# Even attention: where four state-space low parts and four evictions of turned probabilities run

## The reference, cut to what matters

```python
att = swa_sink_attention(q, k, v, sinks, rel_bias) * silu(gate_a)    # 8 heads, window of 128
ssm = s5_mixer(u, ...) * silu(gate_b)                                # state space, then a gated unit
return concatenate([att, ssm]) @ w_out

# inside the attention, for each block of 128 queries
logits = where(mask, q @ k.T * scale + bias, -1e30)
p   = softmax(concatenate([logits, sink]))[..., :-1]
out = p @ v
# inside the mixer
y = gelu(y);  h = y @ glu_w + glu_b
return h[..., :W] * sigmoid(h[..., W:])
```

## Time and profile before

| | us |
|---|---|
| median of 3 runs | 2011.0 (2010.79 to 2011.02) |
| the profiled execution | 2010.99 |
| its span, from first to last instruction | 2009.7 |
| busy: TensorE, VectorE, ScalarE, GpSimd | 1944.4, 1438.2, 882.5, 620.8 |
| mean granted clock of TensorE, of full speed | 0.993 |

### The profile page before, as it was taken

How to read it: one execution, slowest core, us unless ns; L and a number is a source line. 1 busy time by engine, 2 the same in 40 slices (tenths; PEclk the granted TensorE clock), 3 DMA queues, 4 the chain that set the end, 5 groups by cost and what they waited for, 6 DMA issues and landing times.

```text
span 2009.7 us, 24201 instructions
## 1 busy us (share of the span) xinstructions
PE 1944.4 (97%) x9108; PEld 1504.4 (75%) x9108; DVE 1438.2 (72%) x2198; ACT 882.5 (44%) x1573; POOL 620.8 (31%) x428
## 2 busy tenths in 40 slices
PE   8999989999999999999999999999999999999997
PEld 6777867787548787666787887888777877777785
DVE  7668686522379997455357799899997887685639
ACT  5343285333457751545212333544226764352431
POOL 3554410552101122545352000000003673235443
PEclk9999999999999999999999999999999999999999
DMA  6322330442501122311333211111142223455322
GB/s 271 128 72 83 114 123 22 167 158 69 151 22 33 53 76 82 105 42 53 123 98 105 74 54 63 53 53 53 57 147 86 79 74 145 163 191 195 112 85 105
DMA packets 72428, 197.90 MB, mean 98 GB/s; under 512 B 11182, under 2 KB 20559, under 8 KB 71800
## 3 DMA queue, kind: packets, MB, share of 16 engines
q1 hardware_dynamic: 72168, 196.35, 28.9%
q10 hardware_dynamic: 144, 0.00, 0.0%
HBM read 152.89 MB, written 46.71 MB: 99 GB/s over the span
## 4 chain that ended last, share of the span: by engine, by line
PE 47%; DVE 30%; ACT 4%; issue 3%; DMA 2%; POOL 1%; SPq 0%; DVEq 0%; ACTq 0%
PE psum L266 44%; DVE m L2973 10%; DVE m L2187 4%; PE psum L269 3%; DVE m L2994 2%; DVE m L321 2%; DMA m<-in_w 1%; POOL m L311 1%; ACT m L301 1%; DVE m L540 1%; DVE m L456 1%; DVE m L531 1%; DVE m L3172 1%; DVE m L3111 1%; DVE m L3175 1%
## 5 line engine op out<-in xcount | busy, mean ns | idle before, releaser
L266 PE MATMUL psum<-m,m 128*128 128x512 f32 (+10 forms) x8308 | 1862.1, 393 | 40.1 <-DVE m L321 9.8
L266 PEld LDWEIGHTS psum<-m,m 128*128 128x128 f32 (+4 forms) x8308 | 1418.6, 186 | 454.0 <-issue 137.7
L311 POOL TENSOR_TENSOR m<-m,m 128x1024 fp32r<-128x1024 f32 (+1 forms) x122 | 307.9, 2527 | 1002.3 <-ACT m L301 1002.2
L301 ACT ACTIVATE m<-m 128x1024 fp32r<-128x1024 f32 (+2 forms) x166 | 173.4, 1048 | 342.1 <-PE psum L266 208.5
L2973 DVE SCALAR_TENSOR_TENSOR m<-m,m,m 128x1024 f32<-128x1024 f32 x240 | 312.3, 1303 | 6.3
L269 PE MATMUL psum<-m,m 128*128 128x128 f32 x784 | 110.6, 277 | 12.1 <-ACT m L1450 6.1
L269 PEld LDWEIGHTS psum<-m,m 128*128 128x128 f32 x784 | 89.6, 141 | 33.3 <-ACT m L1450 8.0
L2187 DVE TENSOR_SCALAR_CACHE_REDUCE m<-m,m 128x896 bf16<-128x896 f32 (+4 forms) x130 | 102.8, 847 | 1.1
L2519 POOL TENSOR_TENSOR m<-m,m 128x384 f32<-128x384 f32 (+5 forms) x48 | 72.5, 1528 | 55.9 <-DVE m L2311 37.2
L2407 ACT ACTIVATE m<-m,m 128x1024 bf16<-128x1024 f32 (+1 forms) x62 | 64.1, 1035 | 26.4 <-DVE m L2214 26.4
L2311 DVE CUSTOM_DVE_ANT_0 m<-psum,m 128x128 f32<-128x128 f32 (+3 forms) x64 | 48.3, 755 | 37.9 <-PE psum L266 36.7
(11 more groups left out here) (314 smaller groups left out, 1652.9 us busy)
## 6 DMA issues: line engine op xcount, KB each, us to landing
m<-in_w SPq DMA_DIRECT2D x164, 512.0 KB, 3.7
scr_hscr<-m SPq DMA_DIRECT2D x4, 2048.0 KB, 6.6
m<-scr_hscr SPq DMA_DIRECT2D x4, 2048.0 KB, 10.6
scr_turned<-scr_strip SPq DMA_DIRECT2D x8, 575.5 KB, 12.6
m<-in_x SPq DMA_DIRECT2D x4, 1024.0 KB, 7.9
scr_gscr<-m SPq DMA_DIRECT2D x16, 256.0 KB, 4.2
m<-in_x SPq DMA_DIRECT2D x2, 2048.0 KB, 8.8
m<-scr_turned SPq DMA_DIRECT2D x8, 512.0 KB, 4.5
```

The costliest lines, as they stand in the source:

```text
L266: return self.nc.tensor.matmul(out, lhsT, rhs, start=start, stop=stop, skip_group_check=True)
L301: k.nc.scalar.activation(k.hi[SLOT[i]][:, 0:kk * n], k.raw[i % 2][:, 0:kk * n], ACT.Copy).then_inc(*k.up("w_hi", i))
L311: k.nc.gpsimd.tensor_tensor(lo, raw, hi.bitcast(F32), ALU.subtract).then_inc(*k.up("w_lo", i))
```

## The change

Two things are moved.

1. `low_y` goes from VectorE to GpSimd. It was in VectorE's steps 6 to 9, at the end of the step; it is now in GpSimd's loop, in steps 5 to 8, behind the weight panel of step 4. It still waits for `y_hi(m)` of ScalarE.
2. The eviction of block c = 1 of units 4 to 7 goes from ScalarE to VectorE, in steps 6 to 9. There it stands behind `s1b` and ahead of `s3`, and waits for the transposes (`swa_PT_ps`) and for `swa_O` of two units before. ScalarE keeps block 0 of those units, and both blocks of all others.

```diff
+        self.turned_by_dve = [(i - 2, 1) for i in range(6, 10)]
...
 (vector_even)
-    def low_y(m):
-        dve.wait_ge(*at("y_hi", m))
-        V.tensor_tensor(E.YL[:, m], E.YT[m].rearrange("p j c -> p (j c)"), E.YH[:, m].bitcast(F32), ALU.subtract).then_inc(*up("y_lo", m))
+    def s2(b, p):
+        i = E.units.index((b, p))
+        for c in range(E.band(b)[0] // 128):
+            if (i, c) not in E.turned_by_dve:
+                continue
+            dve.wait_ge(*at("swa_PT_ps", b, p, c))
+            dve.wait_ge(*at("swa_O", *E.units[i - 2]))
+            V.tensor_copy(E.PT[i % 2][:, c, :], k.bank(E.PB[(b, p, c)])).then_inc(*up("swa_PT", b, p, c, also=[("free", "ev_PB", b, p, c)]))
...
             s1b(*E.units[i - 1])
+        if 2 <= i <= n + 1:
+            s2(*E.units[i - 2])
         if i >= 3:
             s3(*E.units[i - 3])
-        if i - 1 in E.y_steps:
-            low_y(E.y_steps.index(i - 1))
...
 (scalar_even, s2)
+            if (i, c) in E.turned_by_dve:
+                continue
             act.wait_ge(*at("swa_PT_ps", b, p, c))
...
 (pool_even)
+    def low_y(m):
+        pool.wait_ge(*at("y_hi", m))
+        G.tensor_tensor(E.YL[:, m], E.YT[m].rearrange("p j c -> p (j c)"), E.YH[:, m].bitcast(F32), ALU.subtract).then_inc(*up("y_lo", m))
...
         if E.late_panel(i):
             pool_panel(k, 14 + E.late_panel(i))
+        if i in E.y_steps:
+            low_y(E.y_steps.index(i))
```

## The result

The changed kernel took 2022.0 us (median of 4 executions, 2018.7 to 2023.6) beside 2011.0 for the kernel before (2010.8 to 2012.6): a ratio of 1.0048, 95% interval 1.0036 to 1.0061. The profiled execution took 2023.56.

The account below looks back on a forecast made before the run. TensorE bounds the kernel, but ahead of the gated unit VectorE's steps 6 to 9 set its start; GpSimd's low parts holding VectorE add 3.8 + 1.65 + 1.41 = 6.9 us to 2010.99, giving 2017.9 us, range 2014.5 to 2020.5.

Parts of the forecast that it names:

- the level: Whole kernel: the starting time the forecast adds to, 2010.99 us from the profiled execution, with a median of 2011.0.
- the sum: L1177 of step 9 and the gated unit: 3.8 + 1.65 + 1.41 = 6.9 us later, 2017.9 us; chance 0.54.
- The copy: VectorE, steps 6 to 9: the PSUM copy adds 0.61 us a step, runs beside GpSimd and makes nobody wait.
- Step 6: VectorE: two low parts hold L1188 (L1189 after the change); copy 4.4 us late, step 7's L1177 3.8 late.
- Steps 7 to 9: VectorE: each low part holds L1177 back, 6.35 us a step against 4.70 and 4.94, so 1.65 and 1.41 more.
- without a gap: Kernel before, steps 7 to 9: VectorE never waits, so it sets the step of 4.70 and 4.94 us.
- The turn that passes only at the end of the four: Rival, step 6: GpSimd gets in only after all four L1188; +4.5 us, 2015.5 us; chance 0.15.
- L1189 unheld: Rival, step 6: this one-input operation (L1188 before) is not held; +3.7 us, 2014.7 us; chance 0.08.
- Low parts that hide: Rival, steps 6 to 9: low parts run beside L1170, the copy and L1194; -1.8 us, 2009.2 us; chance 0.08.
- The clock at half in the gated unit's first products: Rival, TensorE from `glu`'s start, turnings too: half clock makes it +9 to 10 us, 2020 to 2021; chance 0.15.
- the hold: VectorE, steps 6 to 9: a low part on GpSimd holds SBUF operations up to 2.27 us, depending on its start.

Follow-up runs that it names:

- the low parts alone: Against the kernel before, only the low parts moved to GpSimd, both evictions left on ScalarE: 2018.1 us, ratio 1.0027.

## Why the prediction was wrong, point by point

**What failed is the last step, the level.** "2010.99 + 6.9 = 2017.9" set the difference on three executions that agreed within 0.23 us; the clock stood in the sum at nothing, and in the range at "up to 2 or 3 us". Those three lay 2.3 us under the mean of 77; an unchanged kernel moves by 10 us between its extremes, with the half-clock stretches that an execution takes; and the four executions of the first comparison lay 0.9 us above the mean of the changed one's 14. The 11.0 us of that comparison against the pooled 7.4 are these things. In the profiled execution the stretches at 63, 391 and 503 us, far from the change, added 4.5 us. No row of one trace could have shown the level, but the earlier trace rows showed that such stretches exist, and I priced the one beside the change and not those of the other 2000 us. The range should have reached some 3 us further up for that alone. Why the first three agreed so well stays open: of the 73 later executions of the kernel before, three picked at random lie within 0.23 us in 0.3% of cases, so it was rare luck or something particular to that first measurement, whose chip isn't on record.

**The difference held, its main term a little high.**
- *The copy*: 0.68 beside GpSimd's work and alone, and without the low parts' move +0.58, +0.59 and +0.35 us in three steps (8.06, 5.29 and 5.29 where 7.48, 4.70 and 4.94 were), with nothing held: as said.
- *Step 6*: the first of the four was held to 290.03, and the low part of 290.17 got its turn between the second and third L1189, as the earlier trace rows had suggested for L1213. Step 6 to 7 took 10.90 us instead of 7.48, +3.4 where I had +3.8: two of the four had run before the second low part's turn, where I had allowed for one or two, and the copy came 4.0 us late, not 4.4.
- *Steps 7 to 9*: 6.33 and 6.32 us where I had 6.35; +1.63 and +1.38 where I had 1.65 and 1.41. (The terms as written, 3.9 + 2.27 + 0.20, make 6.37; the slip is 0.02 us.)
- The sum, 6.43 against 6.9, reached the gated unit in full, and behind it nothing caught up. The held operations are those of the forecast, and the times of the low parts too to 0.5 us, after the 1.45 us by which this execution was late before it; VectorE's busy time went up by 5.0 us.
- *A misreading that cost nothing*: VectorE isn't "without a gap" in the kernel before. In step 8 it waited for TensorE's product, which is most of the 0.24 us by which that step is longer:

```profile
297.03 0.42 DVE L1194 TENSOR_TENSOR m<-psum,m 128x256 f32<-128x256 f32 x1 [0.16 <-PE psum L266]
```

**The rivals.** The turn that passes only at the end of the four fell (it passed after two), and so did L1189 unheld (2.21 us). Low parts that hide are no fault of the idea: with one wait they do hide, and the prediction's figure for that case, -1.8, came out at -1.5 in the trace. What stood against it, that ScalarE's start is tied to L1177 and sets the bad phase anew each step, was right for the change as made. The clock at half in the gated unit's first products did come, in one of three profiles of the changed kernel, and with the size forecast: the stage added 9.2 us there, where I had 9 to 10. It came in one of two profiles of the kernel before as well.

**Where I missed on the way.** I expected the low parts alone to cost almost what the change costs; they cost 2.2 us by step 9. I had taken the hold as 2.27 us whatever ScalarE does ahead of it. Of the 5.1 us by which that kernel was slower, 3.5 are seen behind the stage; the rest is put down to clock stretches only by argument, as is the last microsecond of the changed kernel's 7.4.

Whether the longer waits of TensorE make half clock likelier is shown in part. The mean granted clock was 0.9908 over the changed kernel's 14 executions and 0.9927 over 73 of the kernel before; the difference, 0.0019 give or take 0.0008, is two stretches like that of the earlier trace rows, 1.7 us of clock each. The traces show them in the stage itself: between 289 and 316 us all three of the changed kernel have some 10.2 us at half, the two of before 3.4 and 6.8. There TensorE mostly waits and they cost little unless the gated unit has begun. Between 320 and 1990 us the counts are alike: 5, 4 and 5 against 4 and 5. So the change does bring half clock to its own stage; that it costs anything beyond what the kernel before pays for the same isn't shown.

## What to carry to other kernels

Work moved to an idle GpSimd isn't free when VectorE is the bound, and the price is a question of the start: in the traces of this stage the change cost 6.4 us or gave 1.5, by one wait that put the same four operations beside VectorE's PSUM-reading instructions. Look for such holds in what is there already; a panel's low part, waiting for nothing but its input, cost 2.3 us in the kernel before. And take the level of a kernel from many executions: three that agree to 0.2 us can lie 2 us beside the mean.

## What the runs showed of the hardware that I hadn't expected

- A fill of 128 x 1024 by GpSimd (0.95 us) lets VectorE's two-input operations of 0.16 us run through, where a subtraction of the same size (2.4 us) holds them to its end.
- A waiting GpSimd gets its turn between two VectorE instructions that overlap by 0.08 us: inside one row of four L1189, of 0.35 us each, one took 2.21 and one 2.44 us.
- A held instruction shows as busy time of VectorE, not as a wait: its 128 x 4 operations of 0.16 us read 2.33. In the list of waits nothing stands there.
- One program from execution to execution: spans of 2009.7 and 2013.9 us, and of 2016.9 to 2022.3 for the changed one, by half-clock stretches at places that recur but aren't always taken.
